# Six projection blocks of a hybrid decoder layer as seven quarter products, and the mLSTM query columns in the first stage

## What is computed

```python
def mix_in(x, g_pre, w_in):
    return split_proj(rmsnorm(x, g_pre) @ w_in)   # w_in: 2048 x 8784

IN_SPLITS = (
    ('ml_q', 1024), ('ml_k', 1024), ('ml_v', 1024), ('ml_o', 1024), ('ml_z', 1024),
    ('ml_i', 4), ('ml_f', 4),
    ('sa_q', 512), ('sa_k', 512), ('sa_v', 512), ('sa_z', 512),
    ('idx_q', 512), ('idx_k', 64), ('idx_w', 8),
    ('mem_q', 512), ('mem_z', 512))
```

## Time and profile before

| | |
|---|---|
| time, median of 3 runs | 3199.31 us (3189.67 to 3205.43) |
| time of the profiled execution | 3201.19 us |
| its span | 3199.5 us |
| PE busy | 3025.9 us, 95% of the span |
| DVE, ACT, POOL busy | 1277.6, 463.3, 403.5 us |
| mean granted TensorE clock | 0.972 |

### The profile page before, as it was taken

How to read it: one execution, slowest core, us unless ns; L and a number is a source line. 1 busy time by engine, 2 the same in 40 slices (tenths; PEclk the granted TensorE clock), 3 DMA queues, 4 the chain that set the end, 5 groups by cost and what they waited for, 6 DMA issues and landing times. The chain is left out here.

```text
span 3199.5 us, 32759 instructions
## 1 busy us (share of the span) xinstructions
PE 3025.9 (95%) x11673; PEld 1591.5 (50%) x11673; DVE 1277.6 (40%) x2331; ACT 463.3 (14%) x981; POOL 403.5 (13%) x567
## 2 busy tenths in 40 slices
PE   7899999999998999999999999999689999499998
PEld 5655666544444444444444444444445565255553
DVE  2200100002213799999999755100232231144543
ACT  2100100011104500000000120000122221022221
POOL 0000000002210000000000046100003200133332
PEclk9999999999998899999999999999889999689999
DMA  5333111224424311011202367302255412646542
GB/s 185 125 65 98 57 58 70 102 87 130 131 93 180 101 41 70 34 63 70 73 16 107 113 194 242 109 33 112 96 190 155 127 44 82 199 145 192 187 141 99
DMA packets 228794, 353.27 MB, mean 110 GB/s; under 512 B 37308, under 2 KB 135460, under 8 KB 223404
## 3 DMA queue, kind: packets, MB, share of 16 engines
q1 hardware_dynamic: 187356, 269.85, 25.8%
q0 software_dynamic: 14784, 61.88, 6.3%
q10 hardware_dynamic: 26544, 20.08, 2.1%
HBM read 267.86 MB, written 86.43 MB: 111 GB/s over the span
## 5 line engine op out<-in xcount | busy, mean ns | idle before, releaser
L273 PE MATMUL sbank<-w,xT 128*128 128x512 f32 x2560 | 1102.8, 594 | 7.7 <-ACT pout_b L252 3.2
L273 PEld LDWEIGHTS sbank<-w,xT 128*128 128x128 f32 x2560 | 487.1, 191 | 618.3 <-issue 610.3
L832 PE MATMUL bank<-w,xT 128*128 128x512 f32 (+3 forms) x2048 | 725.2, 514 | 5.6 <-DMA w<-in_w_in 5.6
L832 PEld LDWEIGHTS bank<-w,xT 128*128 128x128 f32 x2048 | 387.2, 191 | 311.5 <-issue 166.1
L1623 PE MATMUL at_bank_bc<-w,at_hT 128*128 128x512 f32 x512 | 230.3, 594 | 3.9 <-ACT at_bc_out L1781 3.9
L644 DVE TENSOR_TENSOR area<-area 128x512 f32<-128x512 f32 (+1 forms) x9 | 6.2, 691 | 487.1 <-DMA area<-in_rot 247.3
L247 ACT ACTIVATE pout_b<-sbank 128x512 f32<-128x512 f32 x80 | 47.4, 598 | 990.1 <-PE sbank L273 990.1
L1269 DVE MATCH_REPLACE8 area<-m,area 128x384 f32<-128x384 f32 (+2 forms) x192 | 165.7, 877 | 0.0
L1266 DVE MAX8 m<-area 128x8 f32<-128x384 f32 (+2 forms) x192 | 155.5, 879 | 11.9 <-DVE area L1269 11.9
L1623 PEld LDWEIGHTS at_bank_bc<-w,at_hT 128*128 128x128 f32 x512 | 95.1, 191 | 103.1 <-issue 101.7
L726 ACT ACTIVATE pout<-bank 128x512 f32<-128x512 f32 (+3 forms) x68 | 35.5, 522 | 585.0 <-PE bank L832 532.0
(11 more groups left out here) (367 smaller groups left out, 2826.8 us busy)
## 6 DMA issues: line engine op xcount, KB each, us to landing
w<-in_w_in SPq DMA_DIRECT2D x26, 2048.0 KB, 12.6
proj<-pout_b SPq DMA_DIRECT2D x80, 256.0 KB, 2.0
area<-in_x_prompt SPq DMA_DIRECT2D x16, 1024.0 KB, 7.3
headT<-area ACTq DMA_DIRECT2D x8, 1024.0 KB, 5.2
area<-roped_q_of_decode POOLq DMA_DIRECT2D x32, 256.0 KB, 4.1
w<-in_w_out SPq DMA_DIRECT2D x4, 2048.0 KB, 18.5
y_of_groups_b_c<-at_bc_out SPq DMA_DIRECT2D x32, 256.0 KB, 2.3
mo_dec_states<-in_state_mlstm_C SPq DMA_DIRECT2D x32, 256.0 KB, 6.4
```

Of the source, the lines that this page charges most:

```text
L273: last = k.nc.tensor.matmul(bank[0:r, 0:self.w], k.xT[:, c, r0:r0 + r], k.w[:, u, c, 0:self.w], start=c == 0, stop=c == KT - 1)
L832: last = nc.tensor.matmul(dst[:, 0:wd], k.xT[:, c, t * P:(t + 1) * P], w[:, b % 2, c, 0:wd], start=c == 0, stop=c == KT - 1)
```

## The change

Six blocks of 512 columns, sa_q, sa_k, mem_q, mem_z and the two halves of ml_q, are computed in `project_rotate` as products of quarters: rows in two halves, contraction in two halves, columns in two halves. In place of eight products of 512 rows x 1024 x 256 columns there are seven, with sums and differences of quarters before and after (Winograd's form of Strassen's scheme). Such a block is called a quad. The two ml_q blocks were in `select` before, which now has eight blocks from C_K on.

- PE: seven phases of four tiles, each tile 8 chunks of 256 columns (16 passes). The decode rows are computed directly, 64 matmuls of 64 columns for each of four quarters in two of the tiles' places.
- DVE: once, sums of quarters of `xT` (`row_sums`, five operations of up to 128x4096); for each quad four sums of weight quarters (128x2048) and 20 sums of 128x256 from PSUM. ACT: eight copies of 128x256 and the decode copy.
- SP: for each quad four quarter loads of 1 MB, 16 stores of 128x256 and four decode stores.
- The other blocks: 296 columns (idx_q's first 288 and the 8 gate columns, in two pieces), memory keys, 296 columns, then the quads, then sa_v, sa_z, memory values. So `load_r`, the rotations and the turned groups lie over sa_v, sa_z and memory values, and begin at chunk 12 of the first tile behind the quads.
- The gather of index keys is issued by POOL ahead of the last rotation, once PE has finished sa_z.
- `ahead` is cut in two: `later` waits for `dots_s` and is called behind six of the last block's stores.

```diff
-B_BLOCKS, B_W = C_I // 512, 512
+B_BLOCKS, B_W = (C_I - C_K) // 512, 512
...
-    BLOCKS = ([(C_I, 344), (C_I + 344, 344), (MEM_K, HW), (MEM_V, HW), (C_I + 688, 344)] +
-              [(C_IQ, 366), (C_IQ + 366, 366), (C_IQ + 732, 364)] + [(C_MZ, 512), (C_SV, 512), (C_SZ, 512)])
+    BLOCKS = [[(C_IQ, 288), (C_I, 8)], [(MEM_K, HW)], [(C_IQ + 288, 296)], [(C_SV, 512)], [(C_SZ, 512)], [(MEM_V, HW)]]
+    QUADS = [C_SQ, C_SK, C_MQ, C_MZ, C_Q, C_Q + 512]
...
         def hooks(m):
...
+            if q >= 2 and q % 2 == 0:
+                found[0] = (q // 2 - 1, 4)
+            if q >= 0 and q % 2 == 0 and q // 2 < N_TILES:
+                found[12] = (q // 2, 0)
+            if q >= 0 and q % 2 == 1:
+                n = q // 2
+                at = (4, 8, 12) if n < QT else (0, 4, 8, 12)
+                found.update({c: (n, g + 1) for g, c in enumerate(at)})
...
+            def quad(n):                                   # SP
+                for t in range(3):
+                    store_quad(n, 0, t)
+                store_quad_decode(n)
+                store_quad(n, 0, 3)
+                sp.wait_ge(w_sums, 4 * n + 4)
+                sp.wait_ge(product, 28 * n + 12)
+                load_next(n, "11")
+                sp.wait_ge(product, 28 * n + 16)
+                load_next(n, "X")
...
+                sp.wait_ge(product, 28 * n + 24)
+                load_next(n, "12")
...
+            for n in range(NQ):
+                quad(n)
+            sp.wait_ge(product, 28 * NQ)
+            for part in range(2):
+                load_w(fp.SZ, part)
+            stores_landed(fp.FIRST[fp.SV])
+            sp.wait_ge(gates.stored, 16 * 8)
+            quads_landed()
+            load_r(0)
+            load_r(1)
...
             for n in range(N_TILES):                       # POOL
+                if n == QT:
+                    pool.wait_ge(k.pti_in, 16)
+                    pool.wait_ge(done, fp.FIRST[fp.LAST])
+                    nc.gpsimd.indirect_dma_start(
+                        out=flat[:, 8192:16384], out_offset=None, in_=ins["cache_kidx"][:, :],
+                        in_offset=bass.IndirectOffsetOnAxis(ap=k.pti[:, 0:1], axis=0)).then_inc(k.pages[0], 16)
                 rotary(pool, nc.gpsimd, order, n, ix, cs2, rix, tb, IDX_H + 1, IDX_D // 2)
...
+            def quad(n):                                   # DVE
...
+                weight_sum(at["X"], at["22"], at["12"], ALU.subtract)
+                if n == 0:
+                    row_sums()
...
+                dve.wait_ge(product, 28 * n + 4)
+                weight_sum(at["11"], at["X"], at["11"], ALU.add)
...
+                dve.wait_ge(product, 28 * n + 8)
+                weight_sum(at["21"], at["21"], at["11"], ALU.subtract)
+                weight_sum(at["12"], at["22"], at["11"], ALU.subtract)
+                for kind, (out, x) in enumerate(((part2, part2), (part3, part2), (qout, part2), (qout, part3), (qout, part2))):
+                    for t in range(4):
+                        dve.wait_ge(product, 28 * n + 4 * (kind + 2) + t + 1)
...
+                        nc.vector.tensor_tensor(out[:, t, :], x[:, t, :], bank[t][:, 0:256], ALU.add).then_inc(sums_read, 1)
...
+            def quad(n):                                   # PE
...
+                for phase, (x, name, first) in enumerate((
+                        (of_x(0, upper), "11", True), (of_x(8, upper), "21", False), (of(rows_b), "11", True),
+                        (of_c, "X", True), (of_x(8, lower), "21", False), (of(rows_a), "12", True),
+                        (of(rows_d), "22", False))):
+                    for t in range(4):
...
+                        for c in range(8):
+                            last = nc.tensor.matmul(bank[t][:, 0:256], x(c, t), at[name][:, c, :],
+                                                    start=first and c == 0, stop=c == 7, skip_group_check=True)
+                        last.then_inc(product, 1)
...
-    pr = Projection(k, "b", B_BLOCKS, B_W, 0)
+    pr = Projection(k, "b", B_BLOCKS, B_W, C_K)
```

More of the change, by code:

```diff
@@ L202, in store_tile, with sync @@
                          self.k.pout[0:r, m % P_BANKS, 0:self.w]).then_inc(self.stored[m % P_BANKS], 16)
-    def sync(self, sp, ahead):
+    def sync(self, sp, ahead, later):
         self.load(sp, 0, 0)
@@ L215, in sync @@
         ahead()
-        self.store(sp, self.n - 1, 1, i)
+        for t in range(N_TILES):
+            if t == P_BANKS:
+                later()
+            self.store_tile(sp, self.n - 1, 1, i, t)
         for j in range(P_BANKS):
@@ L423, in added @@
     def added(self, m):
-        return 64 if self.TILES[m][1] == QT else 16
+        b, t = self.TILES[m]
+        wd = self.WIDTH[b]
+        parts = [self.quarter(wd, j) for j in range(4)] if t == QT else [(0, wd)]
+        return 16 * sum(len(list(self.pieces_of(b, lo, hi))) for lo, hi in parts)
     def stored_by(self, m):
@@ L525, in load_first @@
             def load_first(part):
[L526 to L541, removed]
+                s, dst = weights_of_piece(0, part)
@@ L833, in multiply, with quad_decode @@
                                                 start=c == 0, stop=c == KT - 1)
                 last.then_inc(done, 1)
+            def quad_decode(name, start, stop):
+                c0, h = 8 * int(name[0]) - 8, int(name[1]) - 1
+                for c in range(8):
+                    for j in range(4):
+                        last = nc.tensor.matmul(bank[4][NS * j:NS * (j + 1), 64 * h:64 * h + 64], k.xT[:, c0 + c, SEQ:TOK],
+                                                at[name][:, c, 64 * j:64 * j + 64], start=start and c == 0,
+                                                stop=stop and c == 7, skip_group_check=True)
+                return last
@@ L843, in _ @@
             for m in range(N_TILES, fp.ALL):
-                if m == fp.FIRST[fp.MZ]:
+                if m == fp.FIRST[fp.SV]:
                     pe.wait_ge(copied, N_TILES)
+                    for n in range(NQ):
+                        quad(n)
                 multiply(m, {c: lambda n=n, g=g: turn_group(n, g) for c, (n, g) in hooks(m).items()})
@@ L986, in ahead, with later @@
                                  ).then_inc(k.mvd_in, 16)
+            def later():
                 sp.wait_ge(k.dots_s, 2 + 2 * NS)
@@ L989, in ahead @@
                 sp.dma_start(k.v, outs["prompt_v"].rearrange("(c p) n -> p c n", p=P)).then_inc(k.keys_in, 16)
-            pr.sync(sp, ahead)
+            pr.sync(sp, ahead, later)
         @block.gpsimd
```

306 lines of the change are left out of this document (255 added, 51 removed).

## The result

The changed kernel takes 3159.55 us in the median (3156.40 to 3160.96, 4 runs), the kernel before 3198.30 beside it (3189.67 to 3205.43, 4 runs): ratio 0.9881, 95% interval 0.9855 to 0.9907. I forecast 3144 with a range of 3118 to 3164. The kernel is faster by 1.2%, inside the range, and 15.6 us above the figure. I had forecast 55.8 us less; it is 38.8 less. The profiled execution took 3160.96 us (span 3159.3).

The account below looks back on a forecast made before the run. PE's queue was taken to set the time. Select −228.7, project_rotate +152.4, first block −2, new waits +11.2 and +9.8, stage's end +1.5 sum to −55.8 us: forecast 3144 us, range 3118 to 3164.

Parts of the forecast that it names:

- A quad: In project_rotate: 448 passes of 256 columns at 215.8 ns plus decode rows, 101.0 us against 113.5 for a direct block.
- rival of 256-column passes: In the quads: PE cannot keep 256-column passes at their columns' price, weight loads not all hidden; 3222 at 245 ns; chance 0.03.
- Who feeds the quads: In the quads: DVE's sums, banks, quarter loads and the first quad's row sums all come in time; cost 0.
- rival of waits inside the quads: A phase finds its sum, bank or quarter late; 3186 at 1 us a phase, 3155 for first quad alone; chance 0.13.
- First block: Start of project_rotate: 296 columns in place of 344, partly offset by extra stores and early weights; −2 us (−8 to +4).
- Where the rotations begin: First sa_v tile: rows land behind sa_z's 4 MB of weights, PE waits 8.4 us plus 2.8 of slower clock; +11.2.
- rival in which neither wait arises: Row loads overtake the weights or ACT stores the gather: 3134 us with one wait gone, 3123 with both; chance 0.24.
- The gather: Memory values: the 4 MB gather delays ACT's stores and the last rotation, PE waits 7 us; +9.8 with the clock.
- The turned groups: Over sa_v, sa_z and memory values: 45 groups cost PE 19.9 us beyond matmuls, as in the kernel before.
- The stage's end: End of project_rotate: only 3.4 us of PE work behind the last group, so the barrier comes later; +1.5 us.
- DVE in select: In select: DVE's work ends 1062 us after the stage's start, PE's at 1080; 18 us of room, cost 0.
- rival of `select` as DVE's: DVE rather than PE sets the end of select; 3155 us if 20 us too late; chance 0.05.

Follow-up runs that it names:

- four quads: Changed kernel with only sa_q, sa_k, mq and mz as quads, the two query-column blocks back in the selection: 3187.29 us, ratio 0.9963.
- the changed kernel again: The changed kernel unaltered, run once more as a control: 3160.03 us (3156.25 to 3162.86).
- the three edits of order: Changed kernel with gather behind ninth rotation, row loads one tile later, first two row loads ahead of sa_z's weights: 3128.87 us, ratio 0.9791.

## Why the prediction was right, and by what it was off

The mechanism was right in the main: what the change removes, the price of a quad and both new waits. One step failed, that of the turned groups. That the time lies inside the range is in part luck. The misses up to `select` sum to 23.1 us, and 7.5 unforeseen us behind it took a third of that back; without them the time would lie near 3167, above the range.

*Select loses two blocks, −228.7.* Measured −228.7 (1309.0 to 1080.3); four quads give it back, +228.6.

*A quad, 101.0 us.* A clean one takes 100.9. The price of a pass, of the decode strips and the seven phases were right to 0.1 us; the rival of 256-column passes is refuted (PEld's loads of 190 ns stay hidden behind 215.8). The +4.0 us over six quads are the stalls in quads 0, 2 and 4. The floor of about 25 ns between two matmul starts, from the Trainium skill's page "TensorE: Matmul & The Clock Gate", section "Wait — 56ns, not 53.3ns?", doesn't bind here: 192 passes of 64 columns in four strips took 2.89 us, 15 ns each.

*Who feeds the quads, 0.* Right. Apart from the stalls PE waits for nothing from 225 to 835 us; the rival of waits inside the quads is refuted. DVE's four large sums took 2.29 us each, under the bound of 2.8. The row sums of the first quad were done at 232.1 us, for the forecast 237, and its third phase began at 258.8, so that handover had 27 us of room for 13.

*First block, −2 (−8 to +4).* It came out at +1.8, inside its bounds. The step named the early weights as what takes some back and undersized them: one row tile behind 5.3 MB of them came 4.0 us later than with the weights spread (15.9 for 11.9). Slow passes in the block scatter by as much: memory keys began at 129.4 and at 124.0 with the same program.

*Where the rotations begin, +11.2.* Mechanism and place right; 7.05 us of wait for 8.4, and 2.5 for 2.8 of slow passes. With the next step it refutes the rival in which neither wait arises. Loading the rows ahead of the weights took all of it away.

*The gather, +9.8.* Mechanism right, and shown by moving it. The wait was mis-sized: 10.37 for 7, since the stores landed after 16.1 us and not after the 13.2 of the earlier trace rows; with slow passes 12.7.

*The turned groups, 19.9.* This is the step that failed, +10.6 us. It took the groups' cost of the kernel before as a fixed price for 45 groups. But the change also moved the last group of a row tile to the first chunk of the next tile, and the row loads to the same instant. ACT's store of the turned heads then lands at 9.3 us and not at 5.2, the rotation starts 9.3 to 14.8 us behind its release, and PE waits six times: 9.3 us, with 3.1 us of slow passes. The prediction asked what the moved gather would run into, and didn't ask it of `load_r`. Moving these loads by one tile gave 13 us back. Of the 12.4 us a wait of 1.78 was in the 19.9 already, from the kernel before:

```profile
735.11 0.66 PE L805 MATMUL rbank<-ident_sb,area 128*128 128x128 f32 x4 [1.78 <-DVEq L702]
```

The three steps together are 11.8 of the 13.9 us by which this stretch is off (−1.7, +2.9, +10.6). The other 2 lie at the same waits: from start to start each wait is 0.17 us longer than its idle time shows, and the turned groups behind the waits took 1.2 us more in all.

*The stage's end, +1.5.* It was 3.0. ACT waits for its store of the rotated decode queries (`roped_q_of_decode`) before it copies the last tile: the copy starts at 1147.15, 2.4 us behind PE's last pass, and the sum had no term for that.

*DVE in select, 0.* Its last dots end at 2208.8 us, 1054.6 into the stage (forecast 1062), 26 us before PE. The rival of `select` as DVE's is refuted.

*The rest, 0.* −7.5 us unforeseen, tied to where the query columns are made (the four-quad kernel lacks it), cause open. It hid a third of the 23.1 us.

*The base.* All was summed against an execution of 3201.2 us, 5 to 8 above the medians that more runs of the kernel before gave (3193.4 to 3195.9), with a stall of 5.6 us and some 3 us behind it that not every execution has. Against those medians the change is worth 34 to 36 us, where 55.8 were forecast; from 3193.4 the same sum would have given 3137.6, 22 us too low. The high base, too, helped the forecast.

## What to carry to other kernels

When a change reorders instructions, list every DMA that now leaves within a microsecond or two of another on any queue, not only the large ones: a 1 MB store beside 1.1 MB of row loads cost as much as the 4 MB gather (13.1 and 13.3 us by the medians, the loads at seven rotations and the gather once), and moving the loads by a tile cost nothing. Here 34 us of gain became 73, mostly by order alone. Take two profiled executions of the baseline before summing against one: a wait that one has and the other hasn't is not a gain. Count idle time and slow passes apart: here the first added up over the edits and the second didn't. And this product split into sums could be priced from columns and passes alone, to within 4 of 606 us, as every feeder had tiles of slack.

## What was unexpected of the hardware

A wait can cost beyond itself, and its length doesn't settle how much. In the changed kernel, behind 10.37 us of idle time eight passes took 6.03 us in place of 3.70, behind 3.64 us they took 5.01 in place of 3.60, behind 1.99 us (1024.80) 5.29, and behind 1.76 us (924.41) still 3.60. The same place in the first block, first in the changed kernel again, then in the kernel with the three edits of order, whose programs don't differ up to there:

```profile
41.36 6.96 PE L1062 MATMUL rbank<-w,xT 128*128 128x296 f32 x16 [3.71 <-issue]
```

```profile
41.36 4.22 PE L1061 MATMUL rbank<-w,xT 128*128 128x296 f32 x16 [3.71 <-issue]
```

Behind the same idle time at the same microsecond the granted clock is 0.61 in the mean in one and 1.00 in the other. What decides it isn't shown.

A run of 192 passes of 15 ns stalls PE for 0.9 to 1.9 us in quads 0, 2 and 4, in every execution that has them and at the same passes; in runs of 64 it doesn't. And the longest wait for the gate rows behind `select` was 17.8 to 20.5 us where the two blocks of `proj` were written in `select`, and 13.7 to 17.8 where they were written earlier.
